# Six pairs of split weight slots and four raw slots in place of four and eight

## What is computed

```python
# first block
h = h + hybrid_mixer(rms_norm(h), w_in, w_out)        # gated delta rule (8 heads) beside a gated convolution
h = h + memory_cross_attention(rms_norm(h), rms_norm(mem), w_q, w_k, w_v, w_o)
h = h + square(relu(rms_norm(h) @ w1)) @ w2           # 2048 -> 8192 -> 2048
# second block, modulated by c
sh1, sc1, gt1, sh2, sc2, gt2 = split(silu(c) @ w_mod + b_mod, 6)        # w_mod: 2048 x 12288
csh1, csc1, ... = split(silu(c_ctx) @ w_mod + b_mod, 6)
x = x + gt1 * (concat(latent attention, neighborhood attention, fourier mix) @ w_out)
x = x + gt2 * ((silu(gate) * val) @ w_down)           # gate, val = conv3(h2 @ w_up), 2 x 5632 wide
return rms_norm(x)
```

## Time and profile before

| | |
|---|---|
| median of 3 runs | 2957.13 us (2954.08 to 2960.24) |
| span of the profiled execution | 2953.1 us |
| TensorE busy | 2835.3 us |
| DVE busy | 2087.9 us |
| ACT busy | 1347.1 us |
| mean granted clock of TensorE | 0.983 |
| DMA | 591.58 MB, mean 200 GB/s |
| raw loads, issue to landing | 906, median 4.6 us |
| modraw loads, issue to landing | 192, median 4.3 us |

### The profile page before, as it was taken

How to read it: one execution, slowest core, us unless ns; L and a number is a source line. 1 busy time by engine, 2 the same in 40 slices (tenths; PEclk the granted TensorE clock), 3 DMA queues, 4 the chain that set the end, 5 groups by cost and what they waited for, 6 DMA issues and landing times.

```text
span 2953.1 us, 55230 instructions
## 1 busy us (share of the span) xinstructions
PE 2835.3 (96%) x23848; PEld 2784.8 (94%) x23848; DVE 2087.9 (71%) x2902; ACT 1347.1 (46%) x1698; POOL 5.1 (0%) x13
## 2 busy tenths in 40 slices
PE   7998888999999999999999999999999999999998
PEld 7998888999998999999999999989689999999998
DVE  6988754698886878787687876545457665665665
ACT  4445423344433554444544545445445544544453
POOL 0000000000000000000000000000000000000000
PEclk9999899999999999999999999999999999999999
DMA  5555201577773787777787775534155555556553
GB/s 204 184 171 166 86 1 74 180 255 263 272 279 127 243 303 289 266 287 281 287 298 262 264 255 191 181 126 150 51 179 172 194 195 185 198 200 193 188 191 122
DMA packets 160451, 591.58 MB, mean 200 GB/s; under 512 B 17840, under 2 KB 17840, under 8 KB 159696
## 3 DMA queue, kind: packets, MB, share of 16 engines
q1 hardware_dynamic: 159264, 579.93, 56.7%
q0 software_dynamic: 944, 8.12, 0.7%
HBM read 585.88 MB, written 2.10 MB: 199 GB/s over the span
## 4 chain that ended last, share of the span: by engine, by line
PE 86%; DVE 9%; ACT 2%; issue 1%; DMA 1%; SPq 0%; DVEq 0%; ACTq 0%
PE bank L465 77%; DVE wlo L1494 3%; PE bank L757 1%; DVE ev L1513 1%; DVE modacc L1727 1%; PE bank L501 1%; PE bank L484 1%; ACT whi L935 1%; PE bank L652 1%; PE bank L505 1%; PE bank L644 1%; PE bank L650 1%; DVE modacc L1480 1%; PE bank L729 1%; PE bank L737 0%
## 5 line engine op out<-in xcount | busy, mean ns | idle before, releaser
L465 PE MATMUL bank<-act,whi 128*128 128x256 f32 x10144 | 1761.2, 279 | 42.9 <-DVE wlo L1494 24.8
L465 PEld LDWEIGHTS bank<-act,whi 128*128 128x128 f32 x10144 | 1545.8, 190 | 48.6 <-DVE wlo L1494 22.5
L1494 DVE TENSOR_TENSOR wlo<-raw,whi 128x1024 fp32r<-128x1024 f32 x906 | 1096.0, 1221 | 463.9 <-ACT whi L935 461.9
L465 PE MATMUL bank<-act,wlo 128*128 128x256 f32 x5072 | 1410.8, 278 | 0.0
L935 ACT ACTIVATE whi<-raw 128x1024 fp32r<-128x1024 f32 x906 | 943.1, 1057 | 800.6 <-PE bank L465 799.9
L465 PEld LDWEIGHTS bank<-act,wlo 128*128 128x128 f32 x5072 | 962.1, 190 | 0.0
L465 PE MATMUL bank<-hid,whi 128*128 128x256 f32 x3456 | 590.3, 276 | 1.5 <-DVE wlo L1494 1.5
L465 PEld LDWEIGHTS bank<-hid,whi 128*128 128x128 f32 x3456 | 520.6, 188 | 2.0 <-DVE wlo L1494 1.3
L465 PE MATMUL bank<-hid,wlo 128*128 128x256 f32 x1728 | 477.4, 276 | 0.0
L1480 DVE SCALAR_TENSOR_TENSOR modacc<-modraw,small,modacc 128x512 f32<-128x512 f32 x480 | 348.0, 745 | 15.1 <-DMA modraw<-mods 9.4
L465 PEld LDWEIGHTS bank<-hid,wlo 128*128 128x128 f32 x1728 | 324.7, 188 | 0.0
(11 more groups left out here) (317 smaller groups left out, 1558.4 us busy)
## 6 DMA issues: line engine op xcount, KB each, us to landing
raw<-stream SPq DMA_DIRECT2D x906, 512.0 KB, 4.6
modraw<-mods SPq DMA_DIRECT2D x192, 512.0 KB, 4.3
h<-x_t SPq DMA_DIRECT2D x4, 512.0 KB, 5.8
memV<-mem_t POOLq DMA_DIRECT2D x1, 2048.0 KB, 8.9
tmp<-ctx_t POOLq DMA_DIRECT2D x1, 2048.0 KB, 9.0
out_t<-tmp SPq DMA_DIRECT2D x4, 512.0 KB, 2.6
cz<-catt POOLq DMA_DIRECT2D x1, 1216.0 KB, 13.4
bias<-na_bias POOLq DMA_DIRECT2D x1, 1024.0 KB, 5.2
```

What stands on the lines that cost most here:

```text
L465: mm = pe.matmul(b[:, hf * T:(hf + 1) * T], lhs, rhs, start=(kc == 0 and hf == 0 and n == 0), stop=(kc == ph.chunks - 1 and n == 2), skip_ ...
L1494: ve.tensor_tensor(wlo[:, at % SPL_N, :], raw[:, at % RAW_N, :], whi[:, at % SPL_N, :].bitcast(F32), ALU.subtract).then_inc(split_done, 1)
```

## The change

RAW_N goes from 8 to 4 and SPL_N from 4 to 6, so `raw`, `whi` and `wlo` together keep their 16 slots of memory. LAG and PRE go from 3 to 4. Since phases no longer start at buffer 0, the buffer numbers are taken from the slot's number in the whole stream. SP's loads are written as one loop over all slots, in the same order as before. Four tails, on ACT and on DVE, are put off by one step (`at_end`), so that they stand where they stood, counted from the phase's end. `MOD_AT`, `MOD_N` and the place of the modulation matmuls stay.

```diff
-RAW_N, SPL_N, MOD_N = 8, 4, 2
+RAW_N, SPL_N, MOD_N = 4, 6, 2
-LAG = 3
+LAG = 4
-PRE = 3
+PRE = 4
...
+        def at_end(f):
+
+            return lambda j: f(j - (LAG - 3)) if j >= LAG - 3 else None
+
...
+            def load(n):
+                sp.wait_ge(split_done, n + 1)
+                sp.dma_start(raw[:, n % RAW_N, :], stream[ds(n, 1), :, :].rearrange("a p n -> (a p) n")).then_inc(raw_in[n % RAW_N], 16)
+
+            def load_mod(m):
+                sp.wait_ge(mod_used, m + 1)
+                sp.dma_start(modraw[:, m % MOD_N, :], mods[ds(m, 1), :, :].rearrange("a p n -> (a p) n")
+                             ).then_inc(mod_in[m % MOD_N], 16)
...
+            with_mod = PH["memk"].slot0
+            for n in range(N_SLOTS):
+                load(n)
+                if 0 <= n - with_mod < 16 * MOD_BODIES and (n - with_mod) % 2:
+                    load_mod((n - with_mod) // 2)
...
-                            buf = (ph.slot0 + j) % SPL_N
+                            buf = (ph.slot0 + i * ph.S + j) % SPL_N
...
-            phase("wout", squared, memory_squares, upper_after("wout"))
+            phase("wout", squared, memory_squares, at_end(upper_after("wout")))
...
```

More of the change, by code:

```diff
@@ L84, in phases @@
         if ph.mod:
-            assert (ph.mod == 2) == (mod < MOD_CTX) and ph.S == 2 * RAW_N
+            assert (ph.mod == 2) == (mod < MOD_CTX) and ph.S == 16
         slot += ph.slots
@@ L88, in phases @@
         mod += ph.iters if ph.mod else 0
-        assert ph.iters == 1 or (ph.S % RAW_N == 0 and ph.K % 2 == 0), ph.name
+        assert ph.iters == 1 or ph.K % 2 == 0, ph.name
     return {ph.name: ph for ph in out}, slot
@@ L931, in f @@
                 def f(i, j):
-                    at = ph.slot0 + j
-                    sc.wait_ge(raw_in[at % RAW_N], i * (16 * (ph.S // RAW_N)) + 16 * (at // RAW_N + 1))
-                    sc.wait_ge(slot_used, i * ph.S + (at + 1))
+                    at = ph.slot0 + i * ph.S + j
+                    sc.wait_ge(raw_in[at % RAW_N], 16 * (at // RAW_N + 1))
+                    sc.wait_ge(slot_used, at + 1)
                     sc.activation(whi[:, at % SPL_N, :], raw[:, at % RAW_N, :], ACT.Copy).then_inc(hi_done, 1)
@@ L1186, in gained @@
                 return f
-            phase("wout", squared, memory_squares, upper_after("wout"))
+            phase("wout", squared, memory_squares, at_end(upper_after("wout")))
             phase("memk", to(memK), h_sqrt(8))
-            phase("memv", to(memV, flip=True), gained("norm_xa", 0), upper_after("memv"))
+            phase("memv", to(memV, flip=True), gained("norm_xa", 0), at_end(upper_after("memv")))
             phase("wq", to(tmp))
@@ L1290, in mlp_sqrt @@
                     c.end(var, 1)
-            phase("wo", squared_gained, tail=upper_after("wo"))
+            phase("wo", squared_gained, tail=at_end(upper_after("wo")))
             for r in range(FF1_ROUNDS):
@@ L1406, in _ @@
             phase("nak_c", to(naK[:, :, 1, :]))
-            phase("nav_c", to(naV[:, 1, :, :], flip=True), shifted, upper_after("nav_c"))
+            phase("nav_c", to(naV[:, 1, :, :], flip=True), shifted, at_end(upper_after("nav_c")))
             phase("nak_x", to(naK[:, :, 0, :]))
@@ L1492, in f @@
                         mod_chunk(ph, i, k)
-                    ve.wait_ge(hi_done, i * ph.S + (at + 1))
+                    ve.wait_ge(hi_done, at + 1)
                     ve.tensor_tensor(wlo[:, at % SPL_N, :], raw[:, at % RAW_N, :], whi[:, at % SPL_N, :].bitcast(F32),
@@ L1893, in memory_sums @@
                     ins.then_inc(mem_sum, 1)
-            residual("wout", extra=memory_sums, tail=lower_after)
+            residual("wout", extra=memory_sums, tail=at_end(lower_after))
             phase("memk", nothing, h_norm(7, scores_too=True))
-            phase("memv", nothing, tail=lower_after)
+            phase("memv", nothing, tail=at_end(lower_after))
             phase("wq", nothing)
@@ L1997, in mlp_factor @@
                     chain(ve.tensor_tensor(r_sq[:, 0, :], r_sq[:, 0, :], r_sq[:, 0, :], ALU.mult))
-            residual("wo", tail=lower_after)
+            residual("wo", tail=at_end(lower_after))
             for r in range(FF1_ROUNDS):
@@ L2175, in _ @@
             phase("nak_c", nothing, second_root)
-            phase("nav_c", nothing, rest_normed, lower_after)
+            phase("nav_c", nothing, rest_normed, at_end(lower_after))
             phase("nak_x", nothing, h_normal)
```

## The result

The changed kernel takes **3350.78 us** (median of 4 runs, 3350.28 to 3355.1) against 2956.41 us before (4 runs, 2954.08 to 2960.24): 1.1339 times as long, 95% interval 1.1326 to 1.1352. The forecast was 3190 us, 3080 to 3330. The sign was right, the size was not: 395 us were lost where 234 were forecast, and the time lies outside the range.

A forecast was written before the change was run, and what follows sets the result against it. TensorE, 96% busy, bounds the kernel; in the 24 bodies DVE's loop with late mod loads was to become the bound. 86 + 148 + 5 - 5 = 234 us on 2953.1, plus 4.0 for the runs' median, gave 3190 us, range 3080 to 3330.

The forecast's parts named there:

- L: Time from the end of the split that releases a mod load to usable modraw; forecast 4.65 us for every load.
- third case: One of three load pairs in a quiet queue; its second load landed 5.0 us after its own issue.
- load 8: Mod load due ahead of the next body's split 0; from it to split 1's end, 4.34 us in single bodies.
- Stretch A: memk to wq, six double bodies; at 61.4 us a body on DVE's loop, forecast +86 us.
- Stretch B: wo to w2_3, two double and sixteen single bodies, at 61.4 and 53.6 us a body; forecast +148 us.
- 5 for ctx: The 2 MB of ctx_t that fall into w1_0 were to lengthen a mod load on the loop: +5 us.
- Part 2: Split pairs from four to six, LAG and PRE from 3 to 4; less starving of TensorE outside the bodies, -5 us.
- Part 1: Raw slots from eight to four; mod loads leave later, single bodies 53.6 us against 44.67, double 61.4 against 46.2.
- The gap costs more: Rival: in the bodies L is long as in the third case, 5.4 us, 123 us more: 3315 us; chance 0.18.
- The loads overlap: Rival: mod loads land 3.2 us after issue, L is 3.65 us and 164 us go: 3027 us; chance 0.12.
- It does what it says: Rival: modraw comes in time in the bodies, only Part 2 is left, at most 26 us faster: 2931 us; chance 0.05.
- The signs named beforehand: Expected profile: modraw waits some 400 us, modulation matmuls 61 and 53 to 54 us apart, wlo waits some 200 us.

The follow-up runs named there:

- the first run: The changed kernel with each modraw load issued two raw loads earlier: 2953.55 us, ratio to the kernel before 0.9987.
- the second run: The changed kernel with split pairs back at four and LAG and PRE back at 3, raw slots staying at four: 3354.59 us.
- the last run: The changed kernel with modraw loads two raw loads earlier and a lag of 3 from ckv_c to the phase before wout2: 2945.62 us, ratio to before 0.9961.
- the narrower load ahead: The changed kernel with raw loads of even slots in the 24 bodies bringing only 128 of 1024 columns: 3289.5 us.

## Why the prediction was wrong in its size

**What bounds it, and the mechanism: right.** SP's queue holds a mod load behind a raw load that is now let go late; the loop of DVE and its mod loads becomes the bound in the bodies; the first and the second run show that nothing else is lost. SP waits for the splits there and hardly for modacc, as forecast; the earlier trace rows had it the other way round (1594 to 1662 us):

```profile
SPq L353 <- DVE wlo L1489: 59.9, 19, 7.4
SPq L357 <- DVE modacc L1475: 1.6, 5, 0.3
```

**The step that failed: the size of L, the term of 4.65 us.** It was taken from pairs of loads that left into a quiet queue, "since in the new order no third load is issued right behind them". The sentence asked the wrong question: what matters is the load *ahead* of the pair. Read issue by issue, the time from the raw load's issue to the mod load's landing is, in the single bodies between 1300 and 2050 us:

| the load ahead left | pairs | mean us | median |
|---|---|---|---|
| 3.5 us or more before the pair | 45 | 4.94 | 4.66 |
| 2.8 to 3.5 us before | 5 | 5.25 | 5.55 |
| 1.8 us before | 35 | 6.05 | 6.05 |
| less than 1.4 us before | 12 | 7.74 | 7.78 |

The forecast 4.57 is the median of the first line less 0.1. In double bodies the load ahead leaves 2.46 us before at the least (but for load 1), and there the mean of 39 pairs (600 to 960 us) is 4.84. My own third case, the load issued at 1332.9 us that took 5.0, was there to be asked about, and I put it into a rival.

Put into the loop as the prediction built it, single body: six L are 4 x (4.94 + 0.08) + 2 x (6.05 + 0.08) = 32.3. In place of load 8's L and the 4.34 behind it, 9.0 in all, comes load 1's path: two splits 2.28, then 7.76 from the end of the last split to the landing (the mean of 12 bodies), then chunk and split 1.9, so 11.9. With 21.1 - 4.34 = 16.8 for the rest that is 61.0 us; measured are 61.3 (mean of the last 14). Double body: 22.7 + 6 x 4.92 + 2.28 + 7.8 + 2.55 = 64.9; measured 65.0 (the first five, from the first split of each to that of the next). The loop's own terms, the splits and the chunks, were right to a few tenths; the forecast bodies were 53.6 and 61.4.

**That load 8 was on the loop and load 1 was not** is part of the same step. In the sum, load 8 had its L, and load 1 lay behind "from load 8 to the end of split 1, 4.34" as if it came in time. With one L for both, the two paths were level: load 1 would be there 2.28 + 4.65 = 6.9 us after the end of split 13, and by way of load 8 DVE comes to chunk 2 after 4.65 + 0.47 + 1.13 + 0.75 = 7.0. But load 1's release is the last of three splits in a row, its pair are the fourth and fifth load within 2.7 us, and chunk 2 is due before split 1: its path is 2.28 + 7.76 = 10.0, load 8's 6.0 + 2.35 = 8.4. The chain after 1627.97 above shows it.

**Stretch A**: forecast +86, measured +93.3 at the attention's start, of which -13.7 came from before memk, so +107 of its own: 86 + 6 x 3.6 = 107.6. **Stretch B**: forecast +148 +5 for ctx, measured +282.8. Of the difference 16 x 7.7 = 123 are the single bodies, 2 x 3.6 the double ones: 148 + 123 + 7 = 278. The 4.8 us left are as much as the 5 for ctx, but also as much as executions of one kernel differ, so no run shows that term by itself.

**Missed: the cross attention, +9.8 us.** The work of the attention on DVE stands behind the splits and chunks of the end of wq and the start of wo, and one of these chunks waits for a late mod load. TensorE's own wait for it, between 960 and 1030 us, and before, between 880 and 921 us:

```profile
PE bank L732 <- DVE stat L1918: 10.4, 3, 8.4
...
PE bank L737 <- DVE stat L1923: 3.7, 3, 1.7
```

The longest of them, 8.4 in place of 1.7, makes 6.8 us of the 9.8. Another 1.7 us are lost at the end of the attention, where the matmuls follow each other every 0.43 us in place of 0.22: the granted clock is 0.66 there (1015 to 1020 us) and was 1.00 (913 to 917.5 us).

```profile
1015.00:1020.00 5.00, 4.46 (x13) 3.67 (x14) 0.40 (x1) 0.00 (x0) 0.00 (x0) 0.66 0.02 3
...
913.00:917.50 4.50, 3.43 (x16) 2.96 (x16) 0.92 (x2) 0.00 (x0) 0.00 (x0) 1.00 0.02 4
```

DVE's timeline ahead of the long wait's end (start, us, line, operation, idle before): the last split of wo's start waits behind a late mod load, and the attention's reduction behind it.

```profile
980.16 1.41 DVE L1475 SCALAR_TENSOR_TENSOR modacc<-modraw,small,modacc 128x512 f32<-128x512 f32 x2 [2.17 <-DMA modraw<-mods]
981.49 1.22 DVE L1489 TENSOR_TENSOR wlo<-raw,whi 128x1024 fp32r<-128x1024 f32 x1
982.63 0.42 DVE L1909 TENSOR_REDUCE small<-bank 128x1 f32<-128x256 f32 x1
```

The prediction let stretch B begin with "four slots are split before the attention" and did not ask who waits for those splits.

**Part 2: the size was off, and its sign depends on the place.** Forecast -5; measured -13.7 before memk (-9.2 to -11.9 in six further traces), +7.8 in the second block's attention phases (with the lag-4 wait for ACT above), +1.7 behind them: -4.2 in all. The first run shows it without Part 1's loss: -1.0 us of span. The net was near by cancellation, which is luck. TensorE's wait for the low half fell from 13.3 to 9.7 in 140 to 300 us, from 4.4 to 3.2 in 300 to 600, and from 3.4 to nothing at the start of memk. These are 8.2 of the 13.7 us; the rest is in no wait for the low half, and the prediction looked at nothing else. The 3.4 at the start of memk is one wait more than the "once more" of its -5.

**The rivals.** "The gap costs more", 3315 us, was nearest, and half of it held: L was as in its third case and longer (5.7 us in the mean of all eight loads of a single body). Its other half did not: TensorE's slower matmuls (mean clock 0.92 from 586 to 974 us and from 1029 to 2129 us) did not enter the chain of the bodies, in which TensorE hardly stands (1.3% of it from 1029 to 2129 us); it costs something only where TensorE is on the chain, as the 1.7 us in the attention. "The loads overlap" fell, though it is right for a mod load that leaves first (3.2 to 3.5 us). "It does what it says" is what the first and the last run make of the change, 2953.6 and 2945.6, not 2931.

**The signs named beforehand.** A wait for modraw of some 400 us: 518 and 59 more. Matmuls of the sums 61 and 53 to 54 us apart: 65 and 61, and "bodies of 58 us or more would say that L was too small" is what it says. TensorE's waits for the low half of some 200 us: 258. After w2_3 as before: nearly, 9.5 us more.

## What to carry to other kernels

When a buffer is made shallower, don't ask only whether its own loads still come in time, but which loads stand behind them in the same queue and were let go by the old depth; moving the mod loads up by two places in the queue was worth 397 us of 3351 here. Price a load on such a loop by the state of the queue at its issue, that is by what left in the 2 us ahead of it, and price the loop's densest place (here three releases in a row) by itself, not by a middle value. Where two paths of the loop come out level, a small error in that price decides which one counts. The Trainium skill's advice (DMA: Bandwidth & Descriptors, "Rules for kernel authors") to issue DMAs early and wait for them late is what the first run shows.

## What the runs showed of the hardware

- Two loads of 512 KB 0.37 us apart: the second lands 4.3 us (median of 45; mean 4.6) after its issue when nothing left for 3.5 us before, but 5.7 (mean of 35) when another left 1.8 us before. One case of 5.9: the load ahead, issued at 1617.33 us, landed after 3.3 us, at 1620.65, so it was 1.5 us from its end when the pair left at 1619.13. The pair itself landed late at its end: the share of the DMA engines and the GB/s in the last column fell long before the landings at 1624.1 and 1625.4.

```profile
1621.50:1623.50 2.00, 2.00 (x20) 2.00 (x19) 0.00 (x0) 0.23 (x1) 0.00 (x0) 1.00 0.91 358
...
1623.50:1625.40 1.90, 1.08 (x10) 0.88 (x8) 0.00 (x0) 1.06 (x1) 0.00 (x0) 1.00 0.07 26
```

  (Window; its length; busy us of PE, PEld, DVE, ACT, POOL; granted clock; DMA share; GB/s.) A share of 0.07 is about what one of 16 engines makes. I read it as one part of the load that comes late, and the landing waits for it; the trace doesn't name the engine, and why a part lags when loads follow closely stays open. With the narrower load ahead the mean for such pairs fell by 1.1 us, to that of the pairs with nothing ahead, so it is tied to what left before.
- The Trainium skill (DMA: Bandwidth & Descriptors, "Anatomy of one DMA") puts a DMA issued from GpSimd at about 2.0 us and its bytes over 436 GB/s. An estimate from it is 3.2 us for one load of 512 KB, and the loads that SP issued first into a quiet queue agree: 3.2 us in the earlier trace rows, 3.3 and 3.4 at 1617.33 and 1627.33 us after the change. By itself it has no term for what left 1.8 us before.
- TensorE's holes of 2 to 6 us in each body lowered the mean granted clock of the bodies from 0.99 and 1.00 to 0.92 and made its busy time 141 us longer. From 1594 to 1662 us TensorE stands nowhere in the chain of waits, so there this cost nothing; in the attention, where it does, 1.7 us were lost to it.
